# ScalarE sums the squares of latent heads itself, and both engines copy the turned queries

## The reference

```python
cq, ckv, k_pe = split(h @ w_a)                          # widths 384, 256, 64
q  = (rms_norm(cq, q_a_gain) @ w_qb).reshape(b, s, 8, 192)
kv = (rms_norm(ckv, kv_a_gain) @ w_kvb).reshape(b, s, 8, 256)
k  = concatenate([kv[..., :128], broadcast(k_pe)], -1)  # 128 + 64 = 192 a head
q, k = rms_norm(q, q_gain), rms_norm(k, k_gain)         # over the 192 of a head
q, k = (concatenate([t[..., :128], rope(t[..., 128:], pos)], -1) for t in (q, k))
p = causal_softmax(q @ k.T * 192 ** -0.5)
```

## Time and profile before

| | us |
|---|---|
| median of three runs | 1599.15 |
| profiled execution | 1600.46 |
| its span, first to last instruction | 1598.7 |
| TensorE matmul busy | 1358.4 (85%) |
| VectorE busy | 561.7 (35%) |
| ScalarE busy | 266.1 (17%) |
| GpSimd busy | 104.3 (7%) |
| read from HBM | 510.54 MB, 320 GB/s over the span |

### The profile page before, as it was taken

How to read it: one execution, slowest core, us unless ns; L and a number is a source line. 1 busy time by engine, 2 the same in 40 slices (tenths; PEclk the granted TensorE clock), 3 DMA queues, 4 the chain that set the end, 5 groups by cost and what they waited for, 6 DMA issues and landing times.

```text
span 1598.7 us, 24375 instructions
## 1 busy us (share of the span) xinstructions
PE 1358.4 (85%) x9400; PEld 820.6 (51%) x9400; DVE 561.7 (35%) x1481; ACT 266.1 (17%) x736; POOL 104.3 (7%) x191
## 2 busy tenths in 40 slices
PE   9989998776776777989998857767767999999997
PEld 4445554443343343565564434434434875888843
DVE  3444633222122222562532221221213043577721
ACT  2144211010010011463111100100101133111100
POOL 1312000000000001210100000000001041000000
PEclk9999999899888889999999887988998999999999
DMA  8877999999999999746999999999999821544300
GB/s 304 307 268 273 395 402 421 421 421 421 422 422 422 422 423 399 258 156 228 413 411 421 421 420 420 421 420 420 421 420 360 275 80 53 198 158 158 132 0 27
DMA packets 117190, 512.99 MB, mean 321 GB/s; under 512 B 11872, under 2 KB 46620, under 8 KB 64872
## 3 DMA queue, kind: packets, MB, share of 16 engines
q1 hardware_dynamic: 115376, 507.49, 80.0%
q0 software_dynamic: 1552, 4.06, 0.8%
q10 hardware_dynamic: 168, 0.09, 0.0%
HBM read 510.54 MB, written 1.07 MB: 320 GB/s over the span
## 4 chain that ended last, share of the span: by engine, by line
PE 35%; DMA 12%; SPq 6%; issue 1%; DVE 1%; ACT 1%; POOL 0%; POOLq 0%; DVEq 0%; ACTq 0%
PE bank L2214 10%; SPq L1666 6%; DMA ring<-in_moe_w_up 5%; PE bank L2245 5%; PE bank L1256 5%; DMA BC<-in_moe_w_up 3%; PE bank L1965 3%; DMA ring<-in_moe_w_gate 2%; PE bank L422 2%; PE bank L434 2%; DMA BC<-in_moe_w_gate 2%; PE bank L1243 1%; PE bank L1271 1%; PE bank L530 1%; PE bank L1284 1%
## 5 line engine op out<-in xcount | busy, mean ns | idle before, releaser
L1256 PE MATMUL bank<-ring,hT 128*32 128x256 f32 (+1 forms) x2976 | 302.3, 463 | 153.1 <-DMA ring<-in_moe_w_up 57.6
L1256 PEld LDWEIGHTS bank<-ring,hT 128*32 128x32 f32 (+1 forms) x2976 | 155.6, 133 | 272.5 <-issue 166.2
L1256 PE MATMUL bank<-BC,hT 128*32 128x256 f32 (+1 forms) x1120 | 160.5, 460 | 52.8 <-DMA ring<-in_moe_w_up 31.9
L1515 DVE TENSOR_SCALAR pT<-pT 128x256 f32<-128x256 f32 x34 | 10.0, 294 | 466.7 <-ACT pT L1633 466.7
L2214 PE MATMUL bank<-hT,ring 128*128 128x256 f32 (+1 forms) x768 | 152.9, 362 | 0.0
L2214 PEld LDWEIGHTS bank<-hT,ring 128*128 128x128 f32 x768 | 135.9, 190 | 16.5
L1243 PE MATMUL bank<-A,hn 128*128 128x128 f32 x1088 | 127.2, 275 | 0.0
L1243 PEld LDWEIGHTS bank<-A,hn 128*128 128x128 f32 x1088 | 124.5, 192 | 1.7 <-issue 1.7
L1256 PEld LDWEIGHTS bank<-BC,hT 128*32 128x32 f32 (+1 forms) x1120 | 79.1, 134 | 89.5 <-issue 63.3
L530 PE MATMUL bank<-ring,hT 128*128 128x512 f32 (+4 forms) x352 | 122.0, 507 | 0.3 <-DVE hT L301 0.2
L1284 PE MATMUL bank<-hT,A 128*128 128x512 f32 x256 | 118.4, 605 | 0.0
(11 more groups left out here) (302 smaller groups left out, 1478.3 us busy)
## 6 DMA issues: line engine op xcount, KB each, us to landing
ring<-in_moe_w_up SPq DMA_DIRECT2D x98, 1024.0 KB, 26.6
ring<-in_moe_w_down SPq DMA_DIRECT2D x96, 1024.0 KB, 26.6
ring<-in_moe_w_gate SPq DMA_DIRECT2D x88, 1024.0 KB, 25.6
BC<-in_moe_w_gate SPq DMA_DIRECT2D x40, 1024.0 KB, 24.7
BC<-in_moe_w_up SPq DMA_DIRECT2D x30, 1024.0 KB, 23.8
BC<-in_moe_w_down SPq DMA_DIRECT2D x28, 1024.0 KB, 27.2
ring<-in_w_ada SPq DMA_DIRECT2D x24, 1024.0 KB, 5.8
ring<-in_w_up SPq DMA_DIRECT2D x22, 1024.0 KB, 5.3
```

What stands on the lines that cost most here:

```text
L1256: i = nc.tensor.matmul(GATE[q * cap:(q + 1) * cap, part * FF:(part + 1) * FF], xg[:, c, q * cap:(q + 1) * cap], u[:, c, :], start=(c == 0) ...
```

## The change

`heads_scalar` squares one head at a time and lets ScalarE sum as it squares, straight into the two columns of `stat` that VectorE's reduction used to write: two operations an item of 192 numbers a token instead of one of 384. `sums` and its semaphore `l_ss` are gone. VectorE waits for an item's squares before it starts on it, since its products overwrite the item in place. GpSimd waits for ScalarE's sums and, from the third item on, also for VectorE's products of two items before (it writes the root to the columns that they read). ScalarE waits, from the third item on, for GpSimd's root of two items before. `t4q` is made without `scalar_only`, so that ScalarE copies its odd fills only; VectorE copies the even ones, in its queue behind `heads_vector` and ahead of `t4k.vector`.

```diff
-        l_sq, l_ss, l_rs = shared("head_sq", 16), shared("head_ss", 16), shared("head_rs", 16)
+        l_sq, l_rs = shared("head_sq", 16), shared("head_rs", 16)
...
                 if j >= 2:
-                    act.wait_ge(*l_ss(j - 1))
-                nc.scalar.activation(l_squares(j), x, ACT.Square).then_inc(l_sq.sem, 1)
+                    act.wait_ge(*l_rs(j - 1))
+                for h in range(L_HEADS):
+                    at_sum = 64 + 8 * (j % 2) + h
+                    i = nc.scalar.activation(l_squares(j)[:, h, :], x[:, h, :], ACT.Square,
+                                             accum_out=stat[:, at_sum:at_sum + 1])
+                i.then_inc(l_sq.sem, 1)
...
             for j in range(len(l_items)):
-                pool.wait_ge(*l_ss(j + 1))
+                pool.wait_ge(*l_sq(j + 1))
+                if j >= 2:
+                    pool.wait_ge(*l_qk(j - 1))
...
-            def sums(j):
+            for j, (x, qk, tt) in enumerate(l_items):
                 dve.wait_ge(*l_sq(j + 1))
-                if j >= 2:
-                    dve.wait_ge(*l_rs(j - 1))
-                nc.vector.tensor_reduce(stat[:, 64 + 8 * (j % 2):64 + 8 * (j % 2) + n], l_squares(j), AX,
-                                        ALU.add).then_inc(l_ss.sem, 1)
-            for j, (x, qk, tt) in enumerate(l_items):
-                if tt == 0:
-                    sums(j)
-                    sums(j + 1)
                 rotate(dve, x[:, :, NOPE:], None, ROT, n, qk, tt, t1_, t2_)
...
-        t4q = l_turn("t4q", q_l, 0, scalar_only=True)
+        t4q = l_turn("t4q", q_l, 0)
...
             heads_vector(dve)
+            t4q.vector(dve)
             t4k.vector(dve)
```

## The result

The changed kernel takes 1601.54 us (median of 12 runs, 1599.48 to 1605.67); twelve runs of the kernel before have a median of 1599.51 (1597.2 to 1601.52). The ratio is 1.0018 with a 95% interval of 1.0011 to 1.0026, so the change costs 2.9 us (1.8 to 4.2); the plain difference of the two medians is 2.03. Run again beside the experiments it came out at 1.0034 (1.0021 to 1.0048). It is slower both times, by 0.18% here and by 0.34% there, on the two sides of the 0.2% that the prediction took as its bound.

What follows compares the result with a forecast made beforehand. The bound was the last copy of turned queries and keys, releasing attention and expert weight stream. Copy order gave +2.6 us, half clock raised it to +3.8: 1599.15 + 3.8 = 1602.95, said as 1602.9; 8-in-10 range 1599.0 to 1605.2.

Steps and rivals of the forecast that it cites:

- likeliest case: Whole kernel: the forecast with +3.2 to +4.5 us, time 1602.3 to 1603.7, chance 0.52.
- (a): TensorE gets full clock on resuming or soon after: +2.6 us, time 1601.7; chance 0.24, in-between sizes included.
- Part 1: Head items: sums move to ScalarE, so VectorE ends the heads at 691.3 against 693.71, 2.4 us earlier.
- Part 2: Query turn: VectorE's copies queue behind all heads, TensorE stands from 686.1 to 692.2, release +2.6 us at full clock.
- The clock: Query turn: TensorE resumes at half clock after its rest, raising +2.6 to +3.5 or +3.9; +3.8 us taken.
- the two rows that I weighed: Earlier TensorE rests: full clock back 3.6 us after work resumed (giving +3.5) or 5.2 us (giving +3.9).
- (b): Expert stage: the weight stream absorbs the later release, time within 1 us of 1599.15; chance 0.09.
- One for one: End of the keys' turn: any delay or advance of the release moves everything after it by the same amount.
- (c): VectorE's early finish reaches the keys, query copies cost nothing: 2.4 us faster, time 1596.75; chance 0.07.
- (d): Half clock lasts over all query fills and into the keys' turn: +4.9 us, time 1604.0; chance 0.08.

Runs made afterwards that it cites:

- the run that takes the half clock away: Changed kernel with 7 useless matmuls on TensorE in its rest after query fill 1; +2.7 us (1.3 to 4.2) against the kernel before.
- the delay of 10.57: Kernel before with eight extra VectorE reductions, results unused, between the heads and the keys' turn; +11.5 us (9.6 to 13.6) against before.
- the first of these experiments: Changed kernel with 13 useless 128x512 matmuls on TensorE after query fill 1; +4.5 us (3.0 to 6.1) against the kernel before.

## Why the prediction was right

It said 1602.9, slower; measured is 1601.5, and a cost of 2.9 us (1.8 to 4.2) where it said 3.8. The time alone doesn't show that the forecast was right: 1601.5 lies below its likeliest case (1602.3 to 1603.7) and beside rival (a), which had 1601.7, and 0.18% is just on the "same" side of its own bound of 0.2%. The second measurement (3.4 to 7.7) leans the other way; 3.8 lies in both intervals. What tells the forecast from (a) is the trace and the run that takes the half clock away.

**Part 1** held in its main numbers. The squares are 0.36 apart as said, ScalarE idles 0.29 (said: some 0.3) before a key block, and VectorE's last product ends at 692.17 - 1.01 = 691.16 in the time of before (said: 691.3). Of the two new waits that it had as free of cost, ScalarE's on GpSimd appears nowhere, and GpSimd's on the products ended before its sum was there (687.16 against 688.75), though the profile names a product. GpSimd's second instruction took 0.74 and not the 0.85 of the earlier trace rows, which accounts for the 0.1 by which the heads ended earlier. One reading was off without effect: 686.1 is when both of the first fills were made, not fill 0 alone. That the sums alone bring nothing was implied by it, and the run with them alone shows it.

**Part 2** held as well: the rest was 5.95 (said: about 6), and ended by VectorE's copy, and the two parts undone one at a time put the loss on this one. Moving the copies up in VectorE's queue shortens the stage by 1.6 to 2.2 us; in the time this isn't shown.

**The clock** was the right second term. It came back 3.9 us after work resumed, near the first of the two rows that I weighed (3.6) and not the second (5.2), to which I had leaned; with 3.6 the working gave +3.5 (697.4 + 6.6 is 704.0, so +3.6 by its own sum), and the stage shows +3.47. That the two agree so closely is luck, since its two terms were off against each other: at full clock the stage costs 2.20 (said: 2.6, rival (a)), and the half clock adds 1.27 (said: 0.9). Of the 0.4 too much at full clock, 0.2 is that query fill 2 starts 37.72 us into the stage (692.60 - 654.88) where I had 37.89; the rest lies in the keys' turn, whose length the prediction had taken over from before.

**The rivals.** (a), that the clock doesn't matter, is refuted in the stage: the half clock is there, and 1.27 us go with it. (b), that the stream absorbs it, is refuted for this change: the sharing alone, with 6.02 in the stage, came out as 6.1, and the delay of 10.57 as 11.5. "One for one" was too strong as a rule, since with 13 useless matmuls 7.21 came out as 4.5. (c), a gain for VectorE, would have needed a query copy before its last product; there is none. The half clock wasn't long enough for (d).

**What remains** is the 0.6 us between the two spans, which the prediction hadn't foreseen: it had taken one execution's other places as fixed, while from the first expert load (4.47 later) to the end (0.6) they moved by 3.9 us, more than the change did. Why the times of some versions lie 2 us above their stages and that of one 2.7 below stays open.

## What to carry to other kernels

When work is shared with a second engine, look at what is ahead of it in that engine's queue: a copy that holds a buffer of a shared pair stops the producer and then the first engine too, so half of the work moved to an engine that is late cost more here than all of it on one that was there. An engine's saved time is worth something only with a consumer ready at that moment; here the 2.5 us of VectorE brought nothing (+0.28 in the stage) with the sums alone, and the kernel got faster only when the banks and the split of the fills were changed too. Compare two traces over the edited stage and check that a delay reaches the end with a deliberate one, as the difference of two spans can be mostly other places. One deliberate delay is not enough to count every later change at its full size in the stage.

## What the runs showed of the hardware

A rest of TensorE cost twice here: rests of 2.1 to 8.5 us in this stage were followed by 3 to 7 us of work at half clock, in which a transpose takes 0.21 to 0.22 us (32 in 6.66, 20 in 4.41) and not 0.14 (8 in 1.09). The longer rest didn't bring the longer half clock: it lasted until 4.4 us after work resumed behind a rest of 8.50 (shared copies only), and 6.6 behind one of 2.51 (copies moved up). Useless matmuls in the rest kept the granted clock at 1.00 and shortened the stage by 1.27 us in one kernel and 0.79 in another. A float32 matmul of 512 columns is two instructions of 0.44 us each in the trace (26 in 11.32), which made the first of these experiments fail.
